# A two-block network kernel on one Trainium2 core: the opening loads the input by column halves and its first projection by pieces, and projects dt second

## What is computed

```python
proj = x @ w_in                               # 1024 -> 512 + 1024 + 1536 + 16
u, z, xbc, dt = jnp.split(proj, [c1, c2, c3], axis=-1)
y_pool = multiscale_pool(u, pool_w, pool_scale)
y_ssm = mamba2_ssd(z, xbc, dt, ...)           # conv over time, silu; softplus(dt + dt_bias)
h = jnp.concatenate([y_pool, y_ssm], axis=-1) @ w_out
x = layer_norm(ALPHA * x + h, g, b)           # then a SwiGLU, a second layer with attention,
                                              # a gated short convolution and an MLP
```

## Time and profile before

| | us |
|---|---|
| median of 3 runs | 981.01 |
| lowest and highest | 980.94, 981.77 |
| the profiled execution | 980.15 |
| its span, first to last instruction | 978.3 |
| TensorE busy | 944.3 |
| VectorE busy | 645.9 |
| ScalarE busy | 466.6 |

### The profile page before, as it was taken

The page is one execution under the profiler, slowest core; times in us unless marked ns, Lnnn a source line. Parts: engine busy times, 40 slices in busy tenths (PEclk is TensorE's granted clock), DMA queues, the critical chain, the costliest instruction groups (busy, mean ns, idle before and its releaser), DMA issues.

```text
span 978.3 us, 15123 instructions
## 1 busy us (share of the span) xinstructions
PE 944.3 (97%) x6537; PEld 862.8 (88%) x6537; DVE 645.9 (66%) x737; ACT 466.6 (48%) x577; POOL 62.0 (6%) x79
## 2 busy tenths in 40 slices
PE   6999989999999999999899999999899999999997
PEld 6999879999999799876699989998799989999986
DVE  4976896645454863676659788788866865555554
ACT  6556744434343465755544343445344644444442
POOL 2034000000000000220030001000000000000000
PEclk9999999999999999999999999999999999999999
DMA  9744466565565453412579999995566456566531
GB/s 280 239 131 130 136 205 219 186 195 178 181 203 177 130 173 110 133 44 87 176 283 331 381 317 338 308 348 165 185 198 198 130 175 213 175 194 191 174 128 44
DMA packets 122282, 190.52 MB, mean 195 GB/s; under 512 B 6566, under 2 KB 103080, under 8 KB 119144
## 3 DMA queue, kind: packets, MB, share of 16 engines
q1 hardware_dynamic: 115184, 156.94, 49.5%
q0 software_dynamic: 5616, 31.78, 8.8%
q10 hardware_dynamic: 1416, 0.83, 0.3%
HBM read 188.49 MB, written 1.05 MB: 194 GB/s over the span
## 4 chain that ended last, share of the span: by engine, by line
PE 80%; DVE 10%; ACT 5%; issue 3%; DMA 1%; DVEq 0%; POOL 0%; ACTq 0%
PE PS L565 15%; PE PS L567 15%; PE PS L566 15%; PE PS L572 10%; PE PS L574 9%; PE PS L573 9%; DVE lo L1575 3%; ACT hi L1136 2%; PE PS L699 1%; PE PS L663 1%; DMA raw<-even_w_in 1%; DVE r L1645 1%; ACT hid L1437 1%; DMA sq<-norm_gains 1%; ACT sq L1321 1%
## 5 line engine op out<-in xcount | busy, mean ns | idle before, releaser
L1575 DVE TENSOR_TENSOR lo<-raw,hi 128x2048 fp32r<-128x2048 f32 (+2 forms) x150 | 336.1, 2258 | 168.8 <-ACT hi L1136 168.6
L565 PE MATMUL PS<-x_hi,hi 128*128 128x256 f32 x1320 | 374.4, 284 | 1.9 <-DVE x_lo L1772 1.9
L567 PE MATMUL PS<-x_hi,lo 128*128 128x256 f32 x1320 | 372.3, 282 | 0.0
L566 PE MATMUL PS<-x_lo,hi 128*128 128x256 f32 x1320 | 371.7, 282 | 0.0
L1136 ACT ACTIVATE hi<-raw 128x2048 fp32r<-128x2048 f32 (+2 forms) x150 | 278.1, 1880 | 10.2 <-DMA raw<-even_w_in 8.0
L565 PEld LDWEIGHTS PS<-x_hi,hi 128*128 128x128 f32 x1320 | 251.2, 190 | 4.3 <-DVE lo L1575 2.3
L566 PEld LDWEIGHTS PS<-x_lo,hi 128*128 128x128 f32 x1320 | 251.2, 190 | 1.9 <-issue 0.5
L567 PEld LDWEIGHTS PS<-x_hi,lo 128*128 128x128 f32 x1320 | 251.2, 190 | 0.0
L572 PE MATMUL PS<-hi,hid_hi 128*128 128x512 f32 x352 | 141.2, 401 | 1.1 <-DVE lo L1575 0.7
L574 PE MATMUL PS<-hi,hid_lo 128*128 128x512 f32 x352 | 138.6, 394 | 0.0
L573 PE MATMUL PS<-lo,hid_hi 128*128 128x512 f32 x352 | 138.5, 393 | 0.0
(11 more groups left out here) (280 smaller groups left out, 825.5 us busy)
## 6 DMA issues: line engine op xcount, KB each, us to landing
raw<-ffn_w_gate SPq DMA_DIRECT2D x22, 1024.0 KB, 5.4
raw<-ffn_w_up SPq DMA_DIRECT2D x22, 1024.0 KB, 5.5
raw<-ffn_w_down SPq DMA_DIRECT2D x22, 1024.0 KB, 5.0
raw<-mlp_w_in SPq DMA_DIRECT2D x16, 1024.0 KB, 5.6
raw<-mlp_w_out SPq DMA_DIRECT2D x16, 1024.0 KB, 5.0
sq<-ada_w POOLq DMA_DIRECT2D x12, 1024.0 KB, 6.3
r<-ada_w POOLq DMA_DIRECT2D x12, 1024.0 KB, 7.2
raw<-sc_w_in SPq DMA_DIRECT2D x12, 1024.0 KB, 5.3
```

Source lines behind the costliest of these rows:

```text
L565: pe.matmul(dst, wh, hi, start=start, stop=False, skip_group_check=True)
L566: pe.matmul(dst, wh, lo, start=False, stop=False, skip_group_check=True)
L567: return pe.matmul(dst, wl, hi, start=False, stop=stop_, skip_group_check=True)
L1575: dve.tensor_tensor(split_view("lo", c), split_view("raw", c), split_view("hi", c).bitcast(F32), ALU.subtract)\
```

## The change

The first projection becomes chunk 0 and dt chunk 1. SyncE loads, in this order: columns 0 to 511 of x for all 256 tokens, two pieces of chunk 0, columns 512 to 1023 of x, the other two pieces. TensorE turns the first half of x (8 transposes), does the steps k = 0 to 3 of the first 128 columns of chunk 0, turns the second half, and goes on with k = 4; dt comes after the whole projection. ScalarE and VectorE take a pair of x and a piece of chunk 0 in turns, and dt after them. The two projections keep their PSUM banks (5 and 4). VectorE's bias of dt now waits for the second `chunk_used`. Some semaphores are merged: `eps_set`, `conv_pad`, `qz_zero` and `cv_pad` to `cleared`; `kr_cos`, `qm_cos` and `kr_rot` to `rope_cos`; `a_ready` and `silu_c_ready` to `a_silu_c`, each with the counts to match.

```diff
         first["even"] = len(chunks)
+        col_chunk(E_IN, 8, XBC0 + 1024, 256)
         col_chunk(E_IN, 8, DT0, 16, 8)
-        for c in (XBC0 + 1024, XBC0 + 1280, XBC0, XBC0 + 256, XBC0 + 512, XBC0 + 768, 0, 256, 512, 768, 1024, 1280):
+        for c in (XBC0 + 1280, XBC0, XBC0 + 256, XBC0 + 512, XBC0 + 768, 0, 256, 512, 768, 1024, 1280):
             col_chunk(E_IN, 8, c, 256)
...
-            for t in range(2):
-                sp.dma_start(x_tok[:, t, :], A["x"][0, t * P:(t + 1) * P, :]).then_inc(sem("x_landed"), 16)
-            for c in range(1, n_chunks):
-                if c == 1:
-                    for i in range(4):
-                        ks = slice(2 * i, 2 * i + 2)
-                        sp.dma_start(slot("raw", 1)[:, ks, :], chunks[1][0][:, ks, :])\
-                          .then_inc(raw_landed[slot_of[1]] if i == 3 else sem(f"piece_landed{i}"), 16)
-                    continue
+            def first_weights(i):
+
+                ks = slice(2 * i, 2 * i + 2)
+                sp.dma_start(slot("raw", 0)[:, ks, :], chunks[0][0][:, ks, :])\
+                  .then_inc(raw_landed[slot_of[0]] if i == 3 else sem(f"piece_landed{i}"), 16)
+
+            for n in range(2):
+                sp.dma_start(x_tok[:, :, n * HB:(n + 1) * HB], A["x"][0][:, n * HB:(n + 1) * HB].rearrange("(t p) d -> p t d", p=P))\
+                  .then_inc(sem("x_rest" if n else "x_landed"), 16)
+                first_weights(2 * n)
+                first_weights(2 * n + 1)
+            for c in range(2, n_chunks):
...
+            def turn_input(half_):
+
+                pe.wait_ge(sem("x_rest" if half_ else "x_landed"), 16)
+                for b in (2 * half_, 2 * half_ + 1):
+                    for k in (2 * b, 2 * b + 1):
+                        for t in range(2):
+                            o = (k % 2) * S + t * P
+                            last = pe.transpose(PS[:, b, o:o + P], x_tok[:, t, k * P:(k + 1) * P], ident)
+                    last.then_inc(sem("x_turned"), 1)
+
             def col(c, bank, hi, lo, operand=None, between=None):
...
-                if c != 1:
+                if c:
                     pe.wait_ge(lo_split, c + 1)
...
                     for k in range(kt):
-                        if c == 1 and m == 0 and k == 6:
-                            pe.wait_ge(lo_split, 2)
-                        elif c == 1 and m == 0 and k % 2 == 0:
+                        if c == 0 and m == 0 and k == 4:
+                            turn_input(1)
+                        if c == 0 and m == 0 and k == 6:
+                            pe.wait_ge(lo_split, 1)
+                        elif c == 0 and m == 0 and k % 2 == 0:
                             pe.wait_ge(sem("lo_piece"), k // 2 + 1)
...
             pe.wait_ge(sem("ident_landed"), 16)
-            pe.wait_ge(sem("x_landed"), 32)
...
+            turn_input(0)
 
             base = first["even"]
-            col(base, 4, x_hi, x_lo, (sem("x_lo_ready"), 0))
-            col(base + 1, 5, x_hi, x_lo)
+            col(base, 5, x_hi, x_lo, (sem("x_lo_ready"), 0))
+            col(base + 1, 4, x_hi, x_lo)
...
             act.dma_start(const[:, 0:P], A["consts"][:, 0:P]).then_inc(sem("ident_landed"), 16)
-            act.dma_start(slot("raw", 0), chunks[0][0]).then_inc(raw_landed[slot_of[0]], 16)
+            act.dma_start(slot("raw", 1), chunks[1][0]).then_inc(raw_landed[slot_of[1]], 16)
...
-            split(0)
             for b in range(4):
                 act.wait_ge(sem("x_turned"), b + 1)
                 act.activation(x_hi[:, 2 * b:2 * b + 2, :], bank2(b), ACT.Copy).then_inc(sem("x_hi_ready"), 1)
+                split_piece(b)
             split(1)
...
-            split(0)
             for b in range(4):
                 dve.wait_ge(sem("x_turned"), b + 1)
                 dve.wait_ge(sem("x_hi_ready"), b + 1)
                 dve.tensor_tensor(x_lo[:, 2 * b:2 * b + 2, :], bank2(b), x_hi[:, 2 * b:2 * b + 2, :].bitcast(F32),
                                   ALU.subtract).then_inc(sem("x_lo_ready"), 1)
+                split_piece(b)
             split(2)
             base = first["even"]
-            dve.wait_ge(chunk_used, base + 1)
+            dve.wait_ge(chunk_used, base + 2)
```

More of the change, by code:

```diff
@@ L744, in _ @@
             pe.wait_ge(sem("ident_landed"), 16)
-            pe.wait_ge(sem("x_landed"), 32)
-            for b in range(4):
-                for k in (2 * b, 2 * b + 1):
-                    for t in range(2):
-                        o = (k % 2) * S + t * P
-                        last = pe.transpose(PS[:, b, o:o + P], x_tok[:, t, k * P:(k + 1) * P], ident)
-                last.then_inc(sem("x_turned"), 1)
+            turn_input(0)
             base = first["even"]
-            col(base, 4, x_hi, x_lo, (sem("x_lo_ready"), 0))
-            col(base + 1, 5, x_hi, x_lo)
+            col(base, 5, x_hi, x_lo, (sem("x_lo_ready"), 0))
+            col(base + 1, 4, x_hi, x_lo)
             pe.wait_ge(sem("rows_landed_act"), 16 * 2)
@@ L1126, in split @@
                     c = done[0]
-                    if c == 1:
-                        for i in range(4):
-                            ks = slice(2 * i, 2 * i + 2)
-                            act.wait_ge(raw_landed[slot_of[1]] if i == 3 else sem(f"piece_landed{i}"), 16)
-                            act.activation(slot("hi", 1)[:, ks, :], slot("raw", 1)[:, ks, :], ACT.Copy)\
-                               .then_inc(hi_split if i == 3 else sem("hi_piece"), 1)
-                        done[0] += 1
-                        continue
                     act.wait_ge(raw_landed[slot_of[c]], landed_at[c])
@@ L1137, in split, with split_piece @@
                     done[0] += 1
+            def split_piece(i):
+                ks = slice(2 * i, 2 * i + 2)
+                act.wait_ge(raw_landed[slot_of[0]] if i == 3 else sem(f"piece_landed{i}"), 16)
+                act.activation(slot("hi", 0)[:, ks, :], slot("raw", 0)[:, ks, :], ACT.Copy)\
+                   .then_inc(hi_split if i == 3 else sem("hi_piece"), 1)
+                done[0] = i // 3
             def preload(func):
-                act.wait_ge(sem("eps_set"), 1)
+                act.wait_ge(sem("cleared"), 1)
                 act.activation(table_sb[:, preloads[0]:preloads[0] + 1], eps_sb[:, 0:1], func)
@@ L1261, in _ @@
             act.wait_ge(sem("heads_landed"), 16 * 3)
-            act.activation(head_vec[:, 2:3], head_vec[:, 1:2], ACT.Exp).then_inc(sem("a_ready"), 1)
+            act.activation(head_vec[:, 2:3], head_vec[:, 1:2], ACT.Exp).then_inc(sem("a_silu_c"), 1)
             split(3)
@@ L1564, in split @@
                     c = done[0]
-                    if c == 1:
-                        for i in range(4):
-                            ks = slice(2 * i, 2 * i + 2)
-                            dve.wait_ge(*((hi_split, 2) if i == 3 else (sem("hi_piece"), i + 1)))
-                            dve.tensor_tensor(slot("lo", 1)[:, ks, :], slot("raw", 1)[:, ks, :],
-                                              slot("hi", 1)[:, ks, :].bitcast(F32), ALU.subtract)\
-                               .then_inc(lo_split if i == 3 else sem("lo_piece"), 1)
-                        done[0] += 1
-                        continue
                     dve.wait_ge(hi_split, c + 1)
@@ L1577, in split, with split_piece @@
                     done[0] += 1
+            def split_piece(i):
+                ks = slice(2 * i, 2 * i + 2)
+                dve.wait_ge(*((hi_split, 1) if i == 3 else (sem("hi_piece"), i + 1)))
+                dve.tensor_tensor(slot("lo", 0)[:, ks, :], slot("raw", 0)[:, ks, :],
+                                  slot("hi", 0)[:, ks, :].bitcast(F32), ALU.subtract)\
+                   .then_inc(lo_split if i == 3 else sem("lo_piece"), 1)
+                done[0] = i // 3
             def link(ins):
@@ L2039, in _ @@
                 split(c + 3 + h)
-            dve.wait_ge(sem("cv_pad"), 1)
+            dve.wait_ge(sem("cleared"), 4)
             def short_conv(q):
```

34 lines of the change are left out of this document (17 added, 17 removed).

## The result

| | before | after |
|---|---|---|
| median of 22 runs each, us | 981.09 | 983.34 |
| lowest and highest | 979.03, 983.08 | 981.18, 984.61 |
| ratio, 95% interval | | 1.0020, 1.0013 to 1.0027 |
| the profiled execution | 980.15 | 983.38 |
| its span | 978.3 | 981.5 |

Both kernels were timed together again for the experiments: 981.48 (35 runs) against 982.73 (12 runs), ratio 1.0013 (1.0004 to 1.0022). So the change costs 1.3 to 2.3 us by medians, against 1.1 in the forecast. Both intervals leave out 1, so the changed kernel is slower, by little. The first comparison is twice the forecast and stands where the second rival stood (983.4), the second lies by the forecast; the two profiled executions alone (+3.2 us) would overstate the change.

What follows compares the result with a forecast made beforehand. TensorE, busy 944.3 of 978.3 us, bounds the kernel. Start wins 3.6; low clock 1.1, turns 1.0, waits 2.2 make +0.6; +0.5 at tok and xbc: 981.01 + 1.1 = 982.1 us, range 980.5 to 983.8.

Steps and rivals of the forecast that it cites:

- the second rival: Opening: the clock stays low up to k = 7, +2.4 us, 983.4 us; chance 0.18 together with piece 0 landing late.
- Start: Opening: turns from about 5.02 us, piece 0 landed about 5.4, first matmul at 8.2, 3.6 us earlier than 11.81.
- k = 0 to 3: First projection's first 12 matmuls: from 8.2 to about 10.75 us, at the low level, costing 1.1 us.
- the second turns: The second half's 8 turns, between k = 3 and k = 4: 1.0 us at the high level, 10.75 to 11.75.
- the rise of the level: Opening: TensorE's clock goes from low to high between 9.5 and 11.81 us, put at 10.6.
- the +0.6 of the sum: End of both early projections on TensorE: next slot at 21.15 us against 20.52, +0.6 us.
- The two waits: TensorE idle for splits of the second half: 1.7 us before k = 4, 0.5 before k = 6, 2.2 together.
- dt last: Behind dt's bias and softplus: conv_in 2.3 us later, first convolution from 24.29 to 26.6 us.
- The wait at `tok` and xbc: After projection 7, L799 waits for the tok copy and L810 starts at 58.94 against 58.48 us: +0.5 us.
- No cost elsewhere: Projection 4 keeps 1.0 us spare; loads of the fifth chunk and second constants are covered; renamed semaphores move nothing.

Runs made afterwards that it cites:

- e9: The changed kernel, unaltered, timed again on the same chip as three other runs: median 982.73 us, ratio to before 1.0013.
- e11: The changed kernel, unaltered, a third profile: one execution, 981.80 us.
- e12: The changed kernel, unaltered, a fourth profile: one execution, 982.99 us.
- e10: The kernel before, unaltered, one more profile: one execution, 981.59 us.
- e1: The changed kernel, but TensorE turns both halves of x before the first projection: 980.47 us, ratio to before 0.9991.
- e2: As e1, and both halves of x are loaded ahead of all four pieces: 979.93 us, ratio to before 0.9991.
- e6: The changed kernel with idle matmuls wherever TensorE waits in the opening: 980.76 us, ratio to before 0.9995.
- e7: e2 with the softplus of dt moved behind the first convolution: 979.36 us, ratio to before 0.9979.
- e8: e7 plus 17 idle matmuls ahead of the input and 6 behind its turns: 979.45 us, ratio to before 0.9982.
- e4: The changed kernel with the softplus of dt moved behind the first evacuation into conv_in and the first convolution: 982.20 us, ratio to before 1.0011.
- e5: The kernel before with 17 idle matmuls ahead of the input and 14 between its turns and the first slice: 980.04 us, ratio to before 0.9991.
- e3: The changed kernel plus 12 idle matmuls before k = 4 and 3 before k = 6: 981.96 us, ratio to before 1.0013.

## Why the prediction was nearly right, point by point

The change was forecast at +1.1 us, and the executions gave +1.3 and +2.3 by medians; pairs of profiles, the better pictures and the worse, gave, at the turns of xbc, +1.7 and +1.9 us (e9 and e11 at 59.56 and 59.72 against 57.85) and +1.6 and +1.8 (the first profile and e12 at 61.06 and 61.27 against e10's 59.46).

- **Start.** Turns forecast from 5.02, first matmul at 8.2. Measured 5.03 and 8.20. The 5.03 is in part luck: the forecast hung on the identity at 4.84, which came at 0.74 + 3.0 = 3.7, while the half of x that it had at 4.6 came at 4.9. Piece 0 landed at 6.2, later than the 5.4 taken but in time (6.65 was the limit). The steps that follow one another on ScalarE and VectorE were right to 0.1 us.
- **k = 0 to 3.** All 12 low, 8.20 to 10.93, 0.18 more than the sum; the first matmul, with its fill, takes 0.38 and not 0.216 us.
- **The term that was mis-sized: the second turns.** I put the rise of the level at 10.6 us, the middle of a gap in one profile, and so priced the turns at the high level. It came at about 11.8 or later (12.0 in e12, behind 12.3 in e9 and e11). The first four of them, on which x_hi(2) hangs, took 1.06 and not 0.63 us: x_hi(2) started at 11.98, k = 4 at 14.03 and not 13.47. That k = 4 came late (by 0.56 us, in e9 by 0.52, in e11 by 0.69 with the input ready 0.1 us later) is nearly all of the 0.65 and 0.8 us by which the opening of e9 and e11 (+1.25 and +1.41) exceeds the +0.6 of the sum; the last 0.1 is the fill of the first matmul behind the wait at k = 6 (the next starts after 0.22 us).
- **The two waits.** Forecast 1.7 and 0.5 us. From the end of the last turn's slot (12.1 + 0.12 = 12.2) to k = 4 it was 1.8, and 0.4 before k = 6; in e9 and e11, whose turns ended later, 1.4 and 0.4. Each wait is right to 0.1 or 0.3 us, and so is the reason: the split of a piece whose input was turned only then.
- **The second rival.** Its mechanism, the level staying low or falling again, came true in part of the executions, not as the rival had it (low up to k = 7) but as a new fall at 15.2 us after a first rise: 15 matmuls at 0.213 and not 0.12 us, 1.5 us. Its price was 2.4 us in all; these executions have 3.2 and 3.4 against the better picture of before. But before has slow openings too (e10, 1.6 us), so in the medians it cancels as far as both come equally often, which isn't measured. The forecast's picture had only one level per kernel, and that was wrong for both.
- **dt last.** The first convolution was forecast 2.3 - 0.6 = 1.7 us later, relative to the opening; measured 4.39 - 2.75 = 1.64. The wait at `tok` and xbc: forecast 0.5, measured 0.46.
- **No cost elsewhere.** Right: from 61.06 us to the last matmul the distance between the two profiles changes by 0.02 us. From the turns of xbc to the last matmul it is 914.37 to 914.71 us in the three profiles of before and 914.05 to 914.55 in three of the four of after; the fourth, e9, has 915.34.

So the mechanism was right and two things were luck or left out: the start's 5.03, and a level that is not the same from one execution to the next. In the median of the second comparison the result is the forecast's, in that of the first it is twice as large, and though their intervals overlap, nothing here tells whether the 1.0 us between them is more than chance.

Open: the scatter. All 109 timed runs of before lie between 979.03 and 984.19 us, 5.2 us apart, and the opening's two pictures explain 1.6 of these. e9's profile lost another 0.8 us after its opening (1.71 us behind before at the turns of xbc, 2.52 at the last matmul). Its trace has a granted clock of 0.50 from about 419.3 to 422.7 us, which no other profile of after or before has: at 418.2 it was 0.16 us ahead of e11, at 426.4 1.38 us behind. So low stretches differ from one execution to the next later in the kernel too. Of the 87 executions of before beside the experiments, the 39 with a mean granted clock of 0.996 or less have a median of 982.28 us, the 48 with 0.997 or more 980.79. (This mean leaves out the opening's first low stretch: e10's is 0.998.) e1, e2, e6, e7 and e8 scatter by only 1.1 to 1.5 us (11 or 12 runs each), where before scatters by 4.5 to 4.9 in the same groups (35 runs). The waits of the opening alone don't tell them apart: e1 has one of 2.05 us between its turns, before one of 1.93 ahead of its first matmul. No run settles what makes these late stretches rarer.

## What to carry to other kernels

Bringing an operand in earlier didn't pay here, because the tensor engine then had to do other work and wait in the middle of its stream: count the idle gaps that the new order makes and the work that will run at the low clock between them, and put all preparatory turns ahead of the first matmul (e1, e2). A step whose result nobody needs soon (the softplus) must not stand in an in-order queue ahead of one that is needed, least of all when its input has just been made later. Where a difference is a few us, take several profiles of each kernel and count in each how many instructions ran at the low level before explaining anything; matmul spacing tells the level, the page's clock line doesn't.

## What the runs showed of the hardware

- After a rise, TensorE's level fell again following waits of only 1.64 and 0.23 us by the rows (14.03 and 15.23) with six matmuls between them, and rose again after 15 matmuls. In e4 it fell 0.3 us into the work, after waits of 1.50 and 0.23 us. The same work, in other executions (e9, e11), left it high.
- The rise came at very different distances from the first work: in e10 turns from 6.51 and a rise at 16.0 us; in before turns from 6.24 and high by 11.81; in e6 idle work from 1.21 and a rise between 5.1 and 6.3; in e5 the same idle work from 1.21 to 5.21, then a wait of 1.12 us and 16 turns all low, and a rise behind them.
- A 256-column matmul of float32 starts every 0.213 us at the low level and every 0.12 us at the high one, a factor of 1.78, as for the turns (0.214 and 0.12).
- Filling TensorE's waits with idle matmuls lowered the median of after by 2.0 us and that of before by 1.1 us, and had no price that the medians show (one case each; in e8, where VectorE was the bound, it brought nothing; in e3, where only the waits were filled, the vector turns came 0.4 to 0.5 us behind those of e9 and e11).
